# Expert stage of a decoder layer: gate and up weights in 8 KB rows, an fp32r scatter placed in the next pair's step, the combine weight on h, h made in halves

## The reference, cut to what matters

```python
group_prob = softmax(xt @ wg_r + bg_r); gp, gi = top_k(group_prob, 1)
top_logits, ei = top_k(exp_logits[token, gi], 2)
weights = gp * softmax(top_logits)
combine = sum(one_hot(gi * 4 + ei, 16) * weights)
h = silu(einsum('td,edf->etf', xt, w_gate)) * einsum('td,edf->etf', xt, w_up)
h = h * combine.T[:, :, None]
y = einsum('etf,efd->td', h, w_down)
x = layer_norm(ALPHA * x + y, ln2_g, ln2_b)
```

## Time and profile before

| | us |
|---|---|
| timed, median of 3 runs | 1424.29 |
| timed, lowest and highest | 1422.36, 1425.29 |
| profiled execution, span | 1423.4 |
| PE busy (share of the span) | 1345.4 (95%) |
| DVE busy | 559.5 (39%) |
| ACT busy | 483.1 (34%) |

### The profile page before, as it was taken

How to read it: one execution, slowest core, us unless ns; L and a number is a source line. 1 busy time by engine, 2 the same in 40 slices (tenths; PEclk the granted TensorE clock), 3 DMA queues, 4 the chain that set the end, 5 groups by cost and what they waited for, 6 DMA issues and landing times.

```text
span 1423.4 us, 18028 instructions
## 1 busy us (share of the span) xinstructions
PE 1345.4 (95%) x7212; PEld 962.6 (68%) x7212; DVE 559.5 (39%) x695; ACT 483.1 (34%) x632; POOL 38.6 (3%) x49
## 2 busy tenths in 40 slices
PE   6999999999999999999999799799999999999994
PEld 6989989998888888888888577534343343434331
DVE  3477435456454545545445345601111010210106
ACT  3444344346546454444344233311111111211111
POOL 0000000300000000001000000000000000000002
PEclk9999999999999999999999999899999999999997
DMA  9667556544443444555565758699999999999992
GB/s 314 204 183 246 178 185 199 178 160 152 151 158 131 164 161 159 166 190 170 186 202 181 242 177 295 234 403 397 395 405 388 407 387 406 394 399 401 392 410 95
DMA packets 168778, 364.68 MB, mean 256 GB/s; under 512 B 14528, under 2 KB 20128, under 8 KB 159776
## 3 DMA queue, kind: packets, MB, share of 16 engines
q1 hardware_dynamic: 156944, 354.41, 69.9%
q10 hardware_dynamic: 11792, 9.66, 2.2%
HBM read 361.95 MB, written 2.10 MB: 256 GB/s over the span
## 4 chain that ended last, share of the span: by engine, by line
PE 92%; DVE 3%; ACT 2%; ACTq 1%; issue 1%; DMA 1%; SPq 0%; DVEq 0%
PE main L875 18%; PE main L877 18%; PE main L876 18%; PE main L416 16%; PE att L445 8%; PE att L401 5%; PE main L458 4%; PE att L1100 1%; PE att L1068 1%; ACTq L1464 1%; DMA raw<-in_w_in_dram 1%; ACT whi L1261 1%; DVE wlo L1479 1%; DVE acc L637 1%; PE att L1083 1%
## 5 line engine op out<-in xcount | busy, mean ns | idle before, releaser
L1479 DVE TENSOR_TENSOR wlo<-raw,whi 128x2048 fp32r<-128x2048 f32 (+1 forms) x141 | 324.1, 2299 | 395.4 <-ACT whi L1261 395.4
L1261 ACT ACTIVATE whi<-raw 128x2048 fp32r<-128x2048 f32 (+1 forms) x141 | 269.4, 1911 | 456.3 <-PE main L877 431.1
L416 PE MATMUL main<-mraw,xg 128*64 128x512 f32 x1024 | 225.0, 594 | 0.0
L875 PE MATMUL main<-whi,xhi 128*128 128x512 f32 (+1 forms) x544 | 203.5, 374 | 1.3 <-ACT uT L1300 1.3
L877 PE MATMUL main<-whi,xlo 128*128 128x512 f32 (+1 forms) x544 | 201.8, 371 | 0.0
L876 PE MATMUL main<-wlo,xhi 128*128 128x512 f32 (+1 forms) x544 | 201.5, 370 | 0.0
L875 PE MATMUL main<-xhi,whi 128*128 128x256 f32 (+1 forms) x560 | 160.4, 286 | 5.6 <-DVE wlo L1479 5.6
L416 PEld LDWEIGHTS main<-mraw,xg 128*64 128x64 f32 x1024 | 72.6, 137 | 134.7 <-issue 133.2
L876 PE MATMUL main<-xlo,whi 128*128 128x256 f32 (+1 forms) x560 | 159.6, 285 | 0.0
L877 PE MATMUL main<-xhi,wlo 128*128 128x256 f32 (+1 forms) x560 | 159.5, 285 | 0.0
L445 PE MATMUL att<-mraw,hT 128*64 128x512 f32 x512 | 113.0, 600 | 6.2 <-ACT hT L497 6.2
(11 more groups left out here) (299 smaller groups left out, 1309.5 us busy)
## 6 DMA issues: line engine op xcount, KB each, us to landing
raw<-in_w_in_dram SPq DMA_DIRECT2D x96, 1024.0 KB, 5.1
mraw<-in_expert_w_gate_dram SPq DMA_DIRECT2D x64, 1024.0 KB, 14.2
mraw<-in_expert_w_up_dram SPq DMA_DIRECT2D x64, 1024.0 KB, 14.5
mraw<-in_expert_w_down_dram SPq DMA_DIRECT2D x64, 1024.0 KB, 13.8
raw<-in_w_branch_dram SPq DMA_DIRECT2D x24, 1024.0 KB, 5.1
raw<-in_w_out_dram SPq DMA_DIRECT2D x16, 1024.0 KB, 5.1
xin<-in_x_dram SPq DMA_DIRECT2D x4, 512.0 KB, 5.9
xr<-in_x_dram ACTq DMA_DIRECT2D x1, 2048.0 KB, 8.0
```

The costliest lines, as they stand in the source:

```text
L416: ins = pe.matmul(main[0][half, w, :], xg[:, k, half], unit[:, kk * DE:(kk + 1) * DE], start=(k == 0), stop=(k == KT - 1))
L875: pe.matmul(o, ah, bh, start=start, stop=False, skip_group_check=skip)
L1261: act.activation(whi[:, u % SPLIT, 0:n], raw[:, slot, 0:n], ACT.Copy).then_inc(hi_done, 1)
L1479: dve.tensor_tensor(wlo[:, u % SPLIT, 0:n], raw[:, slot, 0:n], whi[:, u % SPLIT, 0:n].bitcast(F32), ALU.subtract).then_inc(lo_done, 1)
```

## The change

- Gate and up units: partition p gets the rows 4p to 4p + 3 of the 512, one piece of 8 KB. So the width is spread differently over partitions: the weights of `gather` are every fourth column of `xr` in a quarter, and ACT takes the layer norm's factor and offset from a new `gbP`, loaded with the same order by two small DMAs.
- Scatter, for all pairs but the last: ACT copies y to `yhi` in fp32r (rounded), DVE subtracts and stores the rest as `ylo` in fp32r; TensorE multiplies `wsl`, now fp32r, by both and adds them in PSUM. The blocks of pair m are scattered in pair m + 1's step, between its gathers. The block order changes from token half by token half to column block by column block. The last pair keeps the fp32 scatter with `ysb`, which moves to a place in `mraw`.
- `wsl` is now the transpose of `hot` (0 and 1). The combine weight of a slot is the sum of its column of `cmb`: two matmuls against a column of ones, copied to `wc` by ACT; DVE multiplies h by `wc` along with up.
- h: silu, product, transposes and copies in two halves of 256 columns.
- On TensorE the first and the last step stand outside the loop, on ACT and DVE the last one. The register with the loop's count is loaded after the first step.

```diff
-                return rows.rearrange("a (k p) f -> p (a k) f", p=P)
+                return rows.rearrange("a (p k) f -> p a (k f)", p=P)
...
+            for j, name in enumerate(("ln1_g", "ln1_b")):
+                sp.dma_start(gbP[:, j * KT:(j + 1) * KT].rearrange("p (q k) -> p q k", k=4),
+                             A[name][0].rearrange("(q p k) -> p q k", p=P, k=4)).then_inc(gbp_in, 16)
...
+            def gather(q):
+                for k in range(4 * q, 4 * q + 4):
+                    for t in range(T):
+                        rows = xr[:, t, q * 512:(q + 1) * 512].rearrange("p (m k) -> p k m", k=4)[:, k % 4, :]
+                        ins = pe.matmul(att[:, q, k % 4 * P:(k % 4 + 1) * P], rows, hot[:, t, :],
+                                        start=(k % 4 == 0 and t == 0), stop=(t == 1), skip_group_check=True)
+                ins.then_inc(xg_ps, 1)
+
+            def scatter(c, before):
+                pe.wait_ge(y_lo, before * 4 + c + 1)
+                for t in range(T):
+                    n = 2 * c + t
+                    if n >= 2:
+                        pe.wait_ge(sc_free, before * 8 + n)
+                    rows = wsl[:, t * P:(t + 1) * P]
+                    pe.matmul(main[1][:, n % 2, :], rows, yhi[:, c % 2, :], start=True, stop=False)
+                    pe.matmul(main[1][:, n % 2, :], rows, ylo[:, c % 2, :], start=False, stop=True).then_inc(sc_ps, 1)
...
                 pe.wait_ge(hot_ok, 1 + m)
-                pe.wait_ge(sc_free, 1 + m * 8)
+                put(0)
+                gather(0)
+                put(1)
+                gather(1)
+                put(2)
+                gate_up(0)
+                put(3)
+                gather(2)
+                gate_up(1)
+                gather(3)
+                pe.wait_ge(cmb_ok, 1 + m)
+                pe.wait_ge(sc_free, 1 + m * 8)
+                for t in range(T):
+                    pe.transpose(main[1][:, 1, t * P:(t + 1) * P], hot[:, t, :], ident[:])
+                for t in range(T):
+                    ins = pe.matmul(main[1][:, 1, S:S + 2], cmb[:, t, :], ones[:, 0:2], start=(t == 0), stop=(t == 1),
+                                    skip_group_check=True)
+                ins.then_inc(ws_t, 1)
+                gate_up(2)
+                gate_up(3)
+                for j in range(2):
+                    pe.wait_ge(h_ok, 1 + j + m * 2)
+                    if j == 1:
+                        pe.wait_ge(wsl_out, 1 + m)
+                    for f in range(2):
+                        ins = pe.transpose(main[1][:, j, f * P:(f + 1) * P], hh[:, (2 * j + f) * P:(2 * j + f + 1) * P],
+                                           ident[:])
+                    ins.then_inc(ht_ps, 1)
...
+            pe.wait_ge(sc_free, 1)
+            step(None, 0, 0)
+            pe.wait_ge(np_ok, 3)
+            more = pe.value_load(runs[0:1, 2:3], min_val=PAIRS // 2 - 1, max_val=PAIRS // 2 * PASSES - 1)
+            with pe.Fori(0, more) as turn:
                 for h in range(2):
-                    step(turn, h * MU, turn * 2 + h)
+                    step(turn, (h + 1) * MU, turn * 2 + h + 1)
+            step(more, MU, more * 2 + 1)
...
+                    else:
+                        if c >= 2:
+                            act.wait_ge(sc_ps, 2 * (c - 1) + m * 8)
+                        act.activation(yhi[:, c % 2, :], att[:, c, :], ACT.Copy).then_inc(y_hi, 1)
...
+            def gated(m):
+                dve.wait_ge(wsl_out, 1 + m)
+                for j in range(2):
+                    cols = slice(j * 256, (j + 1) * 256)
+                    dve.wait_ge(silu_ok, 1 + j + m * 2)
+                    dve.scalar_tensor_tensor(hh[:, cols], hh[:, cols], wc[:, 0:1], main[0][:, 1, cols], ALU.mult,
+                                             ALU.mult).then_inc(h_ok, 1)
+            def put(m):
+                for c in range(4):
+                    dve.wait_ge(y_hi, 1 + c + m * 4)
+                    dve.tensor_tensor(ylo[:, c % 2, :], att[:, c, :], yhi[:, c % 2, :].bitcast(F32),
+                                      ALU.subtract).then_inc(y_lo, 1)
+                    for b in ([], [0], [1], [2, 3])[c]:
+                        for t in range(T):
+                            add(m, 2 * b + t, t, slice(b * 512, (b + 1) * 512))
```

More of the change, by code:

```diff
@@ L243, in build @@
         bw = at("bw", made["ksT"], [P, KT, NG + NE])
-        wsl, lgT = carve(0, "wsl", [P, S]), carve(0, "lgT", [P, S])
+        wsl, lgT = carve(0, "wsl", [P, S], F32R), carve(0, "lgT", [P, S])
         assert small[0] <= made["ksT"] + 8192
@@ L390, in moe_pe @@
             pe.wait_ge(z_ok, T)
-            turns = pe.value_load(runs[0:1, 0:1], min_val=PAIRS // 2, max_val=PAIRS // 2 * PASSES)
             def landed_unit(turn, r):
-                pe.wait_ge(mlanded[r % MRAW], 16 * (r // MRAW + 1) + turn * (16 * (2 * MU // MRAW)))
-            def step(turn, r0, m):
[L397 to L403, removed]
+                value = 16 * (r // MRAW + 1)
+                pe.wait_ge(mlanded[r % MRAW], value if turn is None else value + turn * (16 * (2 * MU // MRAW)))
+            def gather(q):
[14 more added lines that the diff above has]
+                    pe.matmul(main[1][:, n % 2, :], rows, ylo[:, c % 2, :], start=False, stop=True).then_inc(sc_ps, 1)
+            def step(turn, r0, m):
                 def gate_up(q):
@@ L419, in gate_up, with put @@
                                     ins.then_inc(m_used, 1)
+                def put(c):
+                    if turn is not None:
+                        scatter(c, m - 1)
                 pe.wait_ge(hot_ok, 1 + m)
-                pe.wait_ge(sc_free, 1 + m * 8)
[L423 to L431, removed]
@@ L434, in step @@
                 for f in range(DE // P):
[L435 to L438, removed]
+                    if f % 2 == 0:
+                        pe.wait_ge(ht_out, 1 + f // 2 + m * 2)
                     for a in range(2):
@@ L450, in step @@
                                 ins.then_inc(y_ps, 1)
[L452 to L461, removed]
-                for h in range(2):
-                    step(turn, h * MU, turn * 2 + h)
+            pe.wait_ge(sc_free, 1)
[3 more added lines that the diff above has]
+            with pe.Fori(0, more) as turn:
+                for h in range(2):
+                    step(turn, (h + 1) * MU, turn * 2 + h + 1)
+            step(more, MU, more * 2 + 1)
+            for n, (t, cols) in enumerate(blocks):
+                if t == 0:
+                    pe.wait_ge(y_out, 1 + n)
+                if n >= 2:
+                    pe.wait_ge(sc_free, more * 16 + 8 + n)
+                pe.matmul(main[1][:, n % 2, :], wsl[:, t * P:(t + 1) * P].bitcast(F32), ysb[:, cols],
+                          start=True, stop=True).then_inc(sc_ps, 1)
         def act_tail(act, copy_T):
@@ L482, in act_tail, with pair_step @@
             act.activation(warm[:, 2:3], rowok[:], ACT.Silu)
-            act.wait_ge(np_ok, 2)
-            steps = act.value_load(runs[0:1, 1:2], min_val=PAIRS, max_val=PAIRS * PASSES)
-            with act.Fori(0, steps) as m:
+            act.wait_ge(gbp_in, 32)
+            act.wait_ge(np_ok, 4)
+            less = act.value_load(runs[0:1, 3:4], min_val=PAIRS - 1, max_val=PAIRS * PASSES - 1)
+            def pair_step(m, final):
                 for q in range(4):
@@ L502, in act_tail @@
                         act.wait_ge(m_used, MU + m * MU)
-                    act.activation(ysb[:, c * 512:(c + 1) * 512], att[:, c, :], ACT.Copy).then_inc(y_out, 1)
+                    if final:
+                        act.activation(ysb[:, c * 512:(c + 1) * 512], att[:, c, :], ACT.Copy).then_inc(y_out, 1)
+                    else:
+                        if c >= 2:
+                            act.wait_ge(sc_ps, 2 * (c - 1) + m * 8)
+                        act.activation(yhi[:, c % 2, :], att[:, c, :], ACT.Copy).then_inc(y_hi, 1)
+            with act.Fori(0, less) as m:
+                pair_step(m, False)
+            pair_step(less, True)
             act.activation(warm[:, 3:4], rowok[:], ACT.Sqrt)
@@ L667, in dve_moe @@
                 slot_weights((m + 1) % PAIRS, m + 2)
-                combine(m, False)
-            combine(less, True)
+                gated(m)
+                put(m)
+            gated(less)
+            final_adds(less)
             statistics(less, 4 * T - 1)
```

51 lines of the change are left out of this document (27 added, 24 removed).

## The result

| | us, median (lowest to highest) | span of the profiled execution |
|---|---|---|
| before | 1423.32 (1421.75 to 1425.29) | 1423.4 |
| after | 1441.38 (1440.74 to 1442.08) | 1439.1 |

A forecast was written before the change was run, and what follows sets the result against it. TensorE was taken to set the pace, with DMA 4.9 us behind. Savings to 56.0 us a pair and 24.6 us off DMA let DMA end down matmuls at 1366; plus 27.1 and 0.9 gives 1394 us, range 1388 to 1433.

The forecast's parts named there:

- Gather: TensorE's gather weight loads at a 16-byte step: cost taken as 0; DVE's factor would give 5.2, doubling 7.7 us a pair.
- Rival 1: Strided gather weight loads cost 5.2 to 7.7 us a pair; 1434 us, ends 1427 and 1448; chance 0.25.
- The pair: TensorE's time over one pair of experts: falls from 61.35 to 56.0 us.
- scatter: TensorE's scatter per pair, as 16 fp32r matmuls: 3.63 us instead of 7.65, gain 4.0 us.
- The wait for the last add: The gather's wait at the pair boundary goes as the scatter moves into the next pair: gain 0.77 us a pair.
- cover: Margin at the pair boundary: first xg ready at about 6.2 us, TensorE reaching gate_up(0) at 6.8; 0.6 us.
- h in halves: Between gate and up and down matmuls, 2.93 us becomes 1.9: gain 1.0 us a pair, bounds 0.5 and 1.3.
- Combine weight: Four added TensorE records with weight loads: cost 0.4 us a pair, bounds 0 and 0.8.
- The DMA: Gate and up units with 8 KB rows take 2.49 instead of 2.71 us: 24.6 us off, last landing 1363.3, ending the stage.
- rival 2: The DMA rate of gate and up units does not rise with longer rows; 1419 us, chance 0.05.
- Rival 3: New pair-boundary stall, or partly priced strided load, of 1 to 4.8 us a pair; 1410 us at 3; chance 0.10.

The follow-up runs named there:

- e1: Kernel after with one edit: the gather reads 128 adjacent columns of xr again (tokens do not match weight rows); 1394.83 us, ratio 0.9796.
- e3: Kernel after with 2 KB rows in their old order and the contiguous gather, so TensorE's part alone; 1418.53 us, ratio 0.9965.
- e4: Kernel before with 8 KB gate and up rows only, gather still on adjacent columns (tokens do not match weight rows); 1423.05 us, ratio 0.9995.
- e9: Kernel after with the gather's columns at a step of 12 bytes (wrong columns); 1414.24 us, ratio 0.9925, single run.
- e7: Kernel after, with ACT writing the normalised tokens once in gather order so the gather reads contiguously, computing everything; 1395.56 us, ratio 0.9801.
- e2: Kernel before with 8 KB rows, the gather at a step of 16 bytes and gbP, without TensorE's other parts; 1489.26 us, ratio 1.0458.

## Why the prediction was wrong, and where it was right

**The step that failed** is the one named "Gather": "I take 0 ... this is the choice on which the forecast hangs". The step costs 7.4 us a pair (14.76 against 7.32 in e1). With it the prediction's own sum gives 56.0 + 7.4 = 63.4 us, as measured. Rival 1 held both the mechanism and the place, and its upper end of 7.7 us a pair was the right one. The 1448 us it gave there are some 7 too many: seven times 0.3, and 4.8 from the first pair, whose down matmuls end at 968.79, 2.9 us after the forecast 965.9 and not 7.7. Of these 4.8 us, 2.5 are that the step costs less there: against e1 the first gather loses 7.71 - 6.45 = 1.26 us and the two others 3.9. It begins at a granted clock of 0.50 (908 to 913 us), and at that clock contiguous records are slow too (6.45 / 32 = 0.20 us in e1, 0.241 with the step). The other 2.3 us are not of the step: this execution came to the gather 1.2 us earlier than e1 (908.86 for 910.02), and e1's first pair ends 1.1 us before the forecast.

**Why it was chosen wrong.** Three bounds stood there: 0, DVE's factor of 1.67, and doubling. The nearest row and the rule of the Trainium skill that rival 1 names both pointed up, and I set them aside with the sentence that "no row shows TensorE's weight path bound by its reads". What a load is bound by no row shows, but that was the wrong question. What counted is whether the loads set the gather's pace, and for that there was a row, a window over the gather in the kernel before:

```profile
1158.50:1162.20 3.70, 3.70 (x32) 3.56 (x32) 0.00 (x0) 1.51 (x4) 0.00 (x0) 1.00 1.06 388
```

The weight loads are busy 3.56 of 3.70 us, 96%, while in the earlier trace rows they are busy 12.60 of 30 and 3.30 of 10. PE shows as busy throughout too, so the window alone does not say which of the two paces the other. But a gate or up record has 512 moving columns and takes 13.93 / 64 = 0.22 us; by columns alone the gather's 128 would take some 0.05 us (an estimate), and they take 0.12. So the gather was paced by its loads or close to it, and whatever slows a load there shows. Had the loads been busy a third of the time, as for gate and up, a doubled one might have hidden behind its matmul. That last point no run tested.

**What held, measured in e1, where only the stride is taken away:**
- The pair: 56.0 forecast, 55.84 measured. Luck has a part in that: scatter was forecast at 3.63 and took 4.13, gathers at 7.8 and took 7.32, two misses that cancel (11.43 and 11.45). The first record of the first and of the fourth scatter step shows 0.43 us, and the gather behind a scatter step shows one record less.
- The wait for the last add is gone, and nothing came in its place. The first xg are ready 5.9 us after the down matmuls (ACT's first four of eight, 1080.97 + 1.50 - 1076.59) and gate and up start at 6.56: 0.7 us of cover, 0.6 forecast.
- h in halves: 1.88 us from gate and up to down, 1.9 forecast. DVE's half is 0.49 us instead of 0.37 and the two transposes 0.45 instead of 0.33, balanced by smaller hand-overs.
- Combine weight: 0.34 us, 0.4 forecast.
- The DMA: 421 GB/s, TensorE waiting for it 8.0 us in eight small pieces; last landing 1361.96 for 1363.3; down matmuls end at 1365.75 for 1366; time 1394.8 for 1394. That neither half brings anything alone is shown by e3 (1418.5, and rival 2 had 1419) and e4 (1423.05).

**Rival 2** is refuted: with 8 KB rows the rate is 421 to 424 GB/s. The Trainium skill (DMA: Bandwidth & Descriptors, Specifications) puts full line rate at transfers of 512 bytes or more; these rows show otherwise, 387, 412 and 421 GB/s for rows of 2, 4 and 8 KB, and the measurement decides. **Rival 3** did not come: no new stall at the boundary shows in e1's chain. Its partial price of the stride is what 12 bytes would have cost (e9, 1414 us).

## What to carry to other kernels

When an edit changes how an operand is read, ask of the engine that reads it whether that read path is its limit there: a window over just those instructions and the time of one record say it (here weight loads busy 96%, and 0.12 us for a quarter of the columns that elsewhere take 0.22). If it is, take the price from the nearest row, even of another engine, and not zero (DVE's gave 5.2 us a pair; 7.4 were measured). And a layout that is wanted by a transfer is best paid for once, where the data is made (e7), not at each use (64 loads a pair for eight pairs): 1395.56 us against 1441.38.

## What was not expected of the hardware

- Where fp32 weight loads of 128 columns set the pace, a record takes twice the time at a step of 16 or 32 bytes, half as much again at 12 and nearly no more at 8 (table above).
- The strided load does not follow TensorE's clock. In 908 to 913 us, at a granted clock of 0.50, the loads of the kernel after have a mean of 329 ns, later at 1.00 of 327:

```profile
L404 PEld LDWEIGHTS att<-hot,xr 128*128 128x128 f32 x18 | 4.3, 329 | 2.9 <-DVE runs L628 2.9
...
L404 PEld LDWEIGHTS att<-hot,xr 128*128 128x128 f32 x160 | 38.1, 327 | 2.0 <-issue 1.6
```

  The contiguous ones of the kernel before go from 330 ns (910 to 914 us, 0.50) to 192 (1100 to 1300 us, 1.00):

```profile
L401 PEld LDWEIGHTS att<-hot,xr 128*128 128x128 f32 x15 | 3.3, 330 | 2.9 <-issue 2.9
...
L401 PEld LDWEIGHTS att<-hot,xr 128*128 128x128 f32 x217 | 25.1, 192 | 10.5 <-issue 5.7 <-DVE acc L637 4.8
```

  So whatever limits the strided load does not slow with TensorE's clock. What it is, no run isolates.
- In e2 a stretch of 2.9 us in which TensorE mostly waited was followed, in every second pair, by a stretch at a granted clock of 0.50, worth 1.6 to 1.7 us of down matmuls. The kernel before has the same stretch of 2.9 us in all its eight pairs, and one of them shows it. These windows hold the down matmuls of that pair and of the pair before it:

```profile
1319.85:1335.22 15.37, 15.37 (x65) 5.37 (x65) 0.00 (x0) 1.79 (x3) 0.00 (x0) 0.91 1.04 391
1258.50:1272.45 13.95, 13.95 (x65) 4.55 (x65) 0.00 (x0) 1.79 (x3) 0.00 (x0) 1.00 1.04 386
```

  So 1.4 us of the time before are of this kind, which the sum of the prediction did not count. After the 2.1 us of the kernel after, with h in halves, the windows of its eight pairs all show 1.00. Why one pair of eight in one kernel and every second one in the other stays open.
